# A three-slot weight stream: the low part written over the raw weights, and the transfer that waits for TensorE instead of VectorE

## What is computed

```
for l in range(2):                                    # first program
    x = x + 0.5 * swiglu_ffn(rmsnorm(x), ffn1_w_up, ffn1_w_down)
    x = x + mixer(rmsnorm(x), ...)                    # q, k, v, GLU conv (31 taps), gates, dilated attention
    x = x + 0.5 * swiglu_ffn(rmsnorm(x), ffn2_w_up, ffn2_w_down)
    x = rmsnorm(x)
for l in range(2):                                    # second program
    x = x + w_o @ [fourier_mix(u), windowed_gqa(q, k, v)]   # on rmsnorm(x)
    x = x + w_down @ (silu(gate) * val), gate, val = 3-tap conv of (rmsnorm(x) @ w_up)
```

## Time and profile before

| | us |
|---|---|
| median of 3 runs | 2217.0 |
| lowest, highest | 2215.2, 2221.22 |
| profiled execution | 2226.95 |
| its span, first to last instruction | 2225.2 |
| TensorE matmul busy | 2091.5 (94%) |
| VectorE busy | 1532.1 (69%) |
| ScalarE busy | 1043.5 (47%) |
| moved by DMA | 336.58 MB, mean 151 GB/s |

### The profile page before, as it was taken

How to read it: one execution, slowest core, us unless ns; L and a number is a source line. 1 busy time by engine, 2 the same in 40 slices (tenths; PEclk the granted TensorE clock), 3 DMA queues, 4 the chain that set the end, 5 groups by cost and what they waited for, 6 DMA issues and landing times.

```text
span 2225.2 us, 39274 instructions
## 1 busy us (share of the span) xinstructions
PE 2091.5 (94%) x16056; PEld 1975.8 (89%) x16056; DVE 1532.1 (69%) x2177; ACT 1043.5 (47%) x1351; POOL 0.2 (0%) x4
## 2 busy tenths in 40 slices
PE   6999999999999899999998999997999997999998
PEld 6999987788999899989878889996789997779998
DVE  5555788977655655568889676555757766657776
ACT  4444453465543444444436644443445554445554
POOL 0000000000000000000000000000000000000000
PEclk9999999999999999999999999998999999999999
DMA  5545443314555445544332255542225553215554
GB/s 203 200 172 200 165 142 124 114 67 137 202 187 189 146 156 184 192 175 171 127 119 86 82 195 188 187 176 89 82 76 181 193 183 118 104 39 191 187 175 146
DMA packets 51147, 336.58 MB, mean 151 GB/s; under 512 B 5688, under 2 KB 5688, under 8 KB 14696
## 3 DMA queue, kind: packets, MB, share of 16 engines
q1 hardware_dynamic: 50616, 332.72, 42.4%
q10 hardware_dynamic: 432, 2.46, 0.3%
HBM read 334.11 MB, written 1.05 MB: 151 GB/s over the span
## 4 chain that ended last, share of the span: by engine, by line
PE 74%; DVE 15%; ACT 7%; DMA 2%; issue 2%; DVEq 0%; ACTq 0%; SPq 0%
PE bank L367 22%; PE bank L369 22%; PE bank L368 22%; DVE lo L1237 5%; ACT hi L816 3%; PE bank L391 2%; DMA raw<-in_w 2%; DVE cv L1451 2%; PE bank L494 1%; PE bank L502 1%; PE bank L489 1%; DVE qn L1377 1%; PE bank L518 1%; DVE p_sb L1430 1%; DVE rstd L1249 0%
## 5 line engine op out<-in xcount | busy, mean ns | idle before, releaser
L1237 DVE TENSOR_TENSOR lo<-raw,hi 128x2048 fp32r<-128x2048 f32 (+1 forms) x344 | 721.1, 2097 | 324.0 <-ACT hi L816 323.9
L816 ACT ACTIVATE hi<-raw 128x2048 fp32r<-128x2048 f32 (+1 forms) x344 | 601.7, 1753 | 170.9 <-PE bank L369 132.0
L367 PE MATMUL bank<-n_hi,hi 128*128 128x256 f32 x2112 | 601.0, 285 | 38.5 <-DVE n_lo L1241 33.0
L369 PE MATMUL bank<-n_hi,lo 128*128 128x256 f32 x2112 | 600.9, 285 | 0.0
L368 PE MATMUL bank<-n_lo,hi 128*128 128x256 f32 x2112 | 600.3, 284 | 0.0
L367 PEld LDWEIGHTS bank<-n_hi,hi 128*128 128x128 f32 x2112 | 402.4, 191 | 41.0 <-issue 30.7
L367 PE MATMUL bank<-h_hi,hi 128*128 128x256 f32 x1296 | 384.7, 297 | 28.5 <-DVE h_lo L1241 27.0
L369 PEld LDWEIGHTS bank<-n_hi,lo 128*128 128x128 f32 x2112 | 401.6, 190 | 0.0
L368 PEld LDWEIGHTS bank<-n_lo,hi 128*128 128x128 f32 x2112 | 401.1, 190 | 0.2
L368 PE MATMUL bank<-h_lo,hi 128*128 128x256 f32 x1296 | 373.1, 288 | 0.0
L369 PE MATMUL bank<-h_hi,lo 128*128 128x256 f32 x1296 | 372.6, 288 | 0.0
(11 more groups left out here) (209 smaller groups left out, 2365.4 us busy)
## 6 DMA issues: line engine op xcount, KB each, us to landing
raw<-in_w SPq DMA_DIRECT2D x282, 1024.0 KB, 4.8
raw<-in_w SPq DMA_DIRECT2D x62, 512.0 KB, 3.6
bv<-in_bv SPq DMA_DIRECT2D x2, 768.0 KB
x<-in_x ACTq DMA_DIRECT2D x1, 1024.0 KB, 4.9
mask_in<-in_const SPq DMA_DIRECT2D x2, 512.0 KB
out_x<-x SPq DMA_DIRECT2D x1, 1024.0 KB, 3.9
const<-in_const ACTq DMA_DIRECT2D x1, 791.5 KB, 12.6
prm_all<-in_prm ACTq DMA_DIRECT2D x1, 588.0 KB, 8.7
```

Source lines behind the costliest of these rows:

```text
L367: mm(out, w_hi, a_hi, start=start, stop=False, skip_group_check=True)
L369: return mm(out, w_lo, a_hi, start=False, stop=True, skip_group_check=True)
L816: fn(hi[:, s, 0:w], raw[:, s, 0:w], ACT.Copy).then_inc(sem["hi"], 1)
L1237: v.tensor_tensor(lo[:, s, 0:w], raw[:, s, 0:w], hi[:, s, 0:w].bitcast(F32), ALU.subtract)\
```

## The change

`lo` gets the address of `raw`: the subtraction writes its result over its first operand, and 24 KB per partition (3 slots x 2048 values x 4 bytes) come free; nothing uses them. All buffers behind move down. Since TensorE reads the low part out of that memory until it is done with the chunk, a new transfer into the slot has to wait for `pe` (TensorE has finished chunk c-3) in place of `lo` (VectorE has read it). The counts follow: `pe` starts at 3 on TensorE's side as before, `lo` starts at 0 now. No instruction of any engine is moved against another; SP's 344 waits name another semaphore, and one increment of `lo` on VectorE at the start falls away.

```diff
+    at_raw = state["at"]
     raw = sb("raw", [P, SLOTS, CW], F32)
     hi = sb("hi", [P, SLOTS, CW], F32R)
-    lo = sb("lo", [P, SLOTS, CW], F32R)
+    lo = sb("lo", [P, SLOTS, CW], F32R, at_raw)
...
         def chunk(c, src, half):
 
-            sp.wait_ge(sem["lo"], cnt.up("lo"))
+            sp.wait_ge(sem["pe"], cnt.up("pe"))
             w = CW // 2 if half else CW
             sp.dma_start(raw[:, c % SLOTS, 0:w], src[:, 0:w]).then_inc(load[c % SLOTS], 16)
 
         def ffn_stream(layer, stream, cb, chunks):
             with sp.Fori(0, PAIRS) as i:
-                before = cnt.enter(i, dict(lo=3))
+                before = cnt.enter(i, dict(pe=3))
...
-            cnt.end(layer, dict(lo=CHUNKS1))
+            cnt.end(layer, dict(pe=CHUNKS1))
...
-            cnt.end(layer, dict(lo=CHUNKS2))
+            cnt.end(layer, dict(pe=CHUNKS2))
...
     def pe_program(pe):
-        cnt = Count(dict(lo=SLOTS))
+        cnt = Count({})
...
-        v.sem_inc(sem["lo"], SLOTS)
         split(0)
```

## The result

| | before | after |
|---|---|---|
| median, us | 2219.11 (4 runs, 2215.2 to 2222.96) | 2361.15 (4 runs, 2350.05 to 2371.31) |
| ratio after / before, 95% | | 1.0622 [1.0589, 1.0655] |
| profiled span, us | 2225.2 | 2367.2 |
| TensorE busy, us | 2091.5 | 2146.2 |
| span less TensorE busy, us | 133.7 | 221.0 |

The change makes the kernel 6.2% slower. The forecast was 2319, its range 2275 to 2370: the time lies inside it, 42 us above the forecast. It is also above 2350, the top of the forecast's own case; what holds it is the part of the range that was drawn on towards the rival of 2385. Two of the 23 executions of the kernel before that ran beside the last kernels read 11371 and 10578 us and stand outside every ratio.

A forecast was written before the change was run, and what follows sets the result against it. TensorE bounds the long loops, provided low parts are ready in time. New waits of 87.2 us plus 15 for the clock, 102 in all, took the profiled 2226.95 to 2329, or 2319 us on the median's scale; range 2275 to 2370.

The forecast's parts named there:

- the forecast's own case: Whole kernel: the summed waits plus clock loss, 2319 us, from 2285 to 2350; 68% chance.
- the rival of 2385: The first rival: feed-forward loops stall too, a slot's round missing by 1.0 us, 66 times: 2385 us; 14% chance.
- (b): Query, key and value chunks: late low part delays the rotary sum, TensorE waits 2.45 us; 15.4 a layer, 30.8 us.
- (f): Second program: low parts late at the transform (2.0, twice) and at its last product (2.0, twice): 8 us.
- (c): Norms after feed-forward blocks: the last high part delays ScalarE's squares by 4.9 us, four times: 19.6 us.
- (d): Half chunks: output projections lose 2.7 us four times, the convolution's projection 3.2 twice: 17.2 us.
- (e): Heads of the feed-forward blocks: the second chunk's high part comes late, 2.9 us, four times: 11.6 us.
- (a): Feed-forward loops: cost 0, with least margins of 1.6 and 1.5 us; latency beyond the margin is paid at once.
- (g): TensorE's clock: a drop to 1.2 GHz costs 1.7 us, about 22 new pauses, nothing to 37 us; 15 taken.
- the projections absorb it: Rival in the query and key projections: VectorE's idle time catches up, so 2273 us; 12% chance.
- all is hidden: Rival: two chunks of 5.76 us outlast 9.3 everywhere, or the moved wait was never the last: 2217 us; 3% chance.
- it is faster: Rival at the block heads: spaced transfers bring the first forward, 2.7 us each, four times: 2206 us; 3% chance.

The follow-up runs named there:

- the order experiment: Changed kernel with VectorE's rotary sums, scalings and last additions to v ahead of the low part in query, key and value chunks: 2304.42 us, 1.0394.
- the reorders: Changed kernel with rotary sums ahead of low parts (2304.42 us), last high part behind the third square (2343.96), or both plus low part behind three residuals (2295.45).
- The reorder: Changed kernel with the last high part of the first program's four feed-forward blocks behind the third square on ScalarE: 2343.96 us, 1.0571.
- the kernel with the delayed transfers: Changed kernel with SyncE loading 8 KB and waiting for it before each chunk's transfer in the feed-forward loops: 2372.89 us, 1.0704.
- the repeat: The changed kernel run once more, unaltered: 2360.78 us, 1.0640.
- the separate buffer: Changed kernel with the low part in its own buffer again, only the transfer's wait on TensorE staying: 2350.67 us, 1.0604.

## Why the prediction was right, and where it was not

**The waits, (b) to (f): right in sum, by terms that missed both ways.** TensorE's gaps in the trace, added up between the ends of the chunks, grew by this much from before to after:

| step | forecast, us | measured, us |
|---|---|---|
| (b) query, key, value | 30.8 | 28.9 |
| (c) last down product, norm (first program) | 19.6 | 18.3 |
| (d) half chunks | 17.2 | 23.3 |
| (e) heads of the blocks | 11.6 | 6.7 |
| (f) transforms, last down product (second program) | 8 | 8.5 |
| gate chunks | 0 | 1.4 |
| sum | 87.2 | 87.1 |

That the sums agree to 0.1 us is luck: the terms are off by up to 6 us, and (d) too low and (e) too high cancel.

(b) was found with its period of two chunks (the two waits above lie 18.05 us apart, reckoned were 18.0) and its 2.3 to 2.4 us, and the order experiment took it away. Of the 23.3 in (d) 15.0 are the output projections (10.8 forecast), 5.0 the convolution's (6.4), and 3.3 a wait for VectorE ahead of the transposes of the second program, which no step has. In (d) the fourth chunk of an output projection was to lose 2.4 us; it lost this:

```profile
595.38 0.39 PE L368 MATMUL bank<-h_hi,hi 128*128 128x256 f32 x1 [3.26 <-DVE lo L1238]
```

The next transfer is issued 0.7 us behind its own, and of the two the first landed after 4.4 us and the second after 6.1, where I had reckoned with 3.6 for each. In (e) what came late was the first chunk's weights, one step before the chain that I followed. ScalarE's high part and TensorE's first matmul of the block:

```profile
611.27 1.91 ACT L817 ACTIVATE hi<-raw 128x2048 fp32r<-128x2048 f32 x1 [3.46 <-DMA raw<-in_w]
```

```profile
615.56 0.39 PE L368 MATMUL bank<-n_hi,hi 128*128 128x256 f32 x1 [3.30 <-DVE lo L1238]
```

The head had idled 2.6 us before and idles 4.3 now, so 1.7 each and not 2.9: part of the new wait took the place of the old one.

**(a), the loops: right.** The iterations keep 17.28 us. The margin reads 1.4 to 1.6 us in the first program, where 1.6 was reckoned, and 1.1 to 1.2 in the second, where it was 1.5. The first rival needed 1.0 us more than the margin and did not come about. The step's last sentence, that more latency than the margin is paid at once, has no support: with 1.7 us more TensorE waited some 0.4 us a round, and the iterations kept their length.

**(c): right in size, incomplete in cause.** Of the 4.6 us a block 3.0 to 3.4 stand ahead of the statistics, as the step has it, and 1.2 to 1.6 ahead of the last product, which no sentence of the step has. That product waits for its hidden values, and VectorE scales the last up tile, from which they come, only behind the late low part of the last down chunk: the same pattern once more, and none of the reorders moved it. The reorder took away 10 of the 12.6 us ahead of the statistics; it brought the first square forward by 2.3 to 2.9 us in three blocks and by 1.6 in the first, and VectorE's low part, which I had not looked at, holds the next piece.

**(g), the clock: the term that was mis-sized.** I took 15 us, with 37 as the bound; it measured 55 (TensorE's busy time) to 60 (the mean clock), above even the bound. The number of drops was nearly right: 24 new stretches, and 22 new pauses had been counted. But the counting passed over pauses that lowered the clock as well, such as the one of 2.25 us before 302.8 above; of all pauses over 1 us the trace has 35 before and 71 after. Two steps failed. "A drop costs 1.7" is half of the shortest stretch, 3.4 us; of the 42 stretches nine last 6.8 us and five 10.2, and the 24 new ones together 116 us, 4.8 each, so 2.4 a drop and (209 - 93) / 2 = 58 in all. And "some drops fall where TensorE waits anyway" was used to take 15 of 37 without a row to bear it out: of the 116 us TensorE was busy for 113. With 55 for 15 the forecast becomes 2359; 2361 was measured, twice.

**The transfer's price: the row was the better guide.** With 4.8 and 3.6 us the waits sum to 87.2, and the kernel after has 4.8 and 3.8; the agreement of the sums proves less, since its terms missed by up to 6 us. The Trainium skill, in SBUF - State Buffer, section "The DMA setup-cost knee", has a fixed 2 us and 436 GB/s, by which they would have been some 12 less, an estimate. The runs add a third point: 8 KB land in 1.7 us, 512 KB in 3.5 to 3.8, 1 MB in 4.8. By that rule, again as estimates, it would be 2.0, 3.2 and 4.4. The first half megabyte costs some 2 us and the second 1.0 to 1.3, so a straight line through the two larger ones, which I drew for the small one, misses by 0.7.

**The rivals.** That the projections absorb it, that all is hidden and that it is faster were all refuted by the same lines: 2.1 to 2.4 us on the rotary sum every second chunk, and squares that come later.

## What to carry to other kernels

When a buffer is freed later, the latency itself need not be the price (here the loops hid it): look on each engine for what stands behind the late instruction in program order and needed nothing of it, and move that first (46 to 56 us here, by two lines moved). Count slots by time, not by number: one slot more, bought with the memory that the change frees, lets each transfer start a chunk (5.76 us) earlier, which covers its way from free slot to landing (5.0 us here), and gave 134 of the 139 us back, with no loss left that can be told. And add to TensorE's new pauses what the lowered clock costs behind them: here 55 us on top of 87 of waiting.

## What the hardware showed that was not expected

**TensorE has more than one pace at granted clock 1.00.** A full chunk of 48 matmuls took 5.76 us in some feed-forward blocks and 5.70 in others of the same execution, and which block got which changed from run to run. The matmuls in two stretches of 80 us, both at clock 1.00 and without a pause, in the kernel before:

```profile
100.00:180.00 80.00, 80.00 (x669) 80.00 (x668) 44.38 (x43) 33.43 (x32) 0.00 (x0) 1.00 0.53 184
660.00:740.00 80.00, 80.00 (x677) 80.00 (x676) 45.63 (x42) 33.50 (x33) 0.00 (x0) 1.00 0.53 187
```

That is 669 and 677 in the same time. In the kernel with the delayed transfers the first of them reads:

```profile
100.00:180.00 80.00, 78.56 (x677) 77.71 (x676) 44.72 (x41) 34.60 (x33) 0.00 (x0) 1.00 0.54 185
```

More matmuls in less busy time. There half of the chunks in the loops took 5.44 or 5.65 us, 0.113 to 0.118 us a matmul against 0.119 to 0.120. Less what lies at half clock, TensorE's busy time reads 2052 to 2057 us in the kernels before and after, the repeat, the separate buffer, the reorders and the four slots, and 2026 only in this one: some 29 us that pay for most of the 36.6 of new waits. What sets the pace was not found. In this loop a small stall cost less than its length, and two executions of one kernel differ by up to 2 us a block (33 x 0.06) with the same waits.

**The clock also fell where no wait was new.** In the kernel with four slots the record holds 10.2 us at 0.50 from 1951.3, in the sequence transform of the second program's second layer. Neither its first layer nor the kernel before has that, though from the start of the first transform to the last TensorE never idles for more than 0.15 us at a time in any of them. The kernel after has such a stretch in both layers; its repeat, the same kernel with much the same waits, in neither. Some of the spread of the changed kernel's times, 2350 to 2371, may well come from this, and counting pauses does not forecast it. The stretch, in the kernel with four slots, and the one ahead of it:

```profile
1945.00:1951.30 6.30, 6.27 (x32) 4.50 (x31) 2.91 (x9) 2.56 (x7) 0.00 (x0) 1.00 0.27 83
```

```profile
1951.30:1961.50 10.20, 10.06 (x39) 8.19 (x38) 3.74 (x12) 3.31 (x11) 0.00 (x0) 0.51 0.01 2
```

TensorE was busy for 6.27 of the 6.30 us before it, and for nearly all of the stretch itself.
